# Where key pages, value pages and rows are turned in a decoder layer's attention: inside the projection and the convolutions, or behind them

## The reference

```python
u = modulate(x, 1)
u_pool, q, k_c, v_c, k_s, v_s, k_w, v_w, g_raw = jnp.split(u @ p['w_in'], splits, axis=-1)
kc_full = jnp.concatenate([kc_past, k_c], axis=1)      # past: pages gathered through page_table
vc_full = jnp.concatenate([vc_past, v_c], axis=1)

def compress(k_full, w1, w2, cmp_pos):     # blocks of 32 rows, stride 16
    h = lax.conv_general_dilated(lhs, w_blk, (STRIDE,), 'VALID', dimension_numbers=('NWC', 'WIO', 'NWC'))
    h = h + jnp.einsum('ld,ldh->h', cmp_pos, w_blk)
    return jax.nn.gelu(h) @ w2
```

## Time and profile before

| | us |
|---|---|
| median of 3 runs (lowest, highest) | 1333.18 (1328.6, 1333.52) |
| the profiled execution | 1331.85 |
| its span, first to last instruction | 1330.2 |
| mean granted TensorE clock, share of full | 0.985 |
| input projection, chunks 2 to 14 | 522.9 to 605.5 |
| from there to the end of the value convolution | 605.5 to 670.6 |
| attention loop | 674 to 762 |

### The profile page before, as it was taken

One profiled execution on the slowest core, in us unless ns is written; L12 is line 12 of the kernel. 1 busy time (PEld: TensorE's weight loads), 2 busy tenths in 40 slices (PEclk: granted clock), 3 DMA queues, 4 the chain that ended last, 5 costly groups with the idle time before them and its releaser, 6 DMA issues.

```text
span 1330.2 us, 25199 instructions
## 1 busy us (share of the span) xinstructions
PE 1278.6 (96%) x9736; PEld 1151.1 (87%) x9736; DVE 569.9 (43%) x969; ACT 439.7 (33%) x681; POOL 188.4 (14%) x372
## 2 busy tenths in 40 slices
PE   5999999999999999998988999989999999999997
PEld 3899999999999998996656667979999999988875
DVE  2532222222333366215577775683332332332466
ACT  3322222222211135226456654252222222223343
POOL 3000000000000026552380060142000000030000
PEclk9999999999999998999999999989999999999999
DMA  9545454454342237863740074512223223364463
GB/s 300 157 123 162 127 174 142 133 181 127 108 163 87 79 105 152 183 141 92 225 122 2 12 209 132 174 34 81 80 83 90 79 79 90 90 195 133 147 197 129
DMA packets 217369, 170.15 MB, mean 128 GB/s; under 512 B 47048, under 2 KB 198904, under 8 KB 217225
## 3 DMA queue, kind: packets, MB, share of 16 engines
q1 hardware_dynamic: 210657, 151.37, 39.4%
q0 software_dynamic: 6640, 17.82, 4.7%
HBM read 164.75 MB, written 8.63 MB: 130 GB/s over the span
## 4 chain that ended last, share of the span: by engine, by line
PE 88%; DVE 5%; ACT 3%; issue 1%; DVEq 1%; DMA 1%; SPq 0%; ACTq 0%
PE ps L326 60%; PE ps L925 10%; PE ps L301 3%; PE ps L2472 2%; ACT AR L1868 1%; PE ps L1158 1%; PE ps L1656 1%; PE ps L1765 1%; PE ps L282 1%; DVE AR L2505 1%; PE ps L1673 1%; DVE AR L2033 1%; PE ps L2671 1%; PE ps L1209 1%; PE ps L388 1%
## 5 line engine op out<-in xcount | busy, mean ns | idle before, releaser
L326 PE MATMUL ps<-UH,WH 128*128 128x288 f32 x1648 | 354.6, 296 | 1.0 <-DVE WL L259 1.0
L326 PE MATMUL ps<-UL,WH 128*128 128x288 f32 x1648 | 350.9, 294 | 0.0
L326 PE MATMUL ps<-UH,WL 128*128 128x288 f32 x1648 | 350.3, 293 | 0.0
L259 DVE TENSOR_TENSOR WL<-RAW,WH 128x1024 fp32r<-128x1024 f32 x134 | 164.9, 1231 | 326.4 <-ACT WH L255 322.8
L326 PEld LDWEIGHTS ps<-UH,WH 128*128 128x128 f32 x1648 | 262.9, 188 | 7.4 <-issue 6.2
L326 PEld LDWEIGHTS ps<-UL,WH 128*128 128x128 f32 x1648 | 264.7, 187 | 0.0
L326 PEld LDWEIGHTS ps<-UH,WL 128*128 128x128 f32 x1648 | 263.5, 188 | 0.0
L255 ACT ACTIVATE WH<-RAW 128x1024 fp32r<-128x1024 f32 x134 | 140.8, 1051 | 140.7 <-PE ps L326 134.8
L925 PE MATMUL ps<-WH,H 128*128 128x512 f32 x380 | 97.3, 398 | 0.0
L691 DVE TENSOR_TENSOR T<-MU,ps 128x576 f32<-128x576 f32 x44 | 33.2, 754 | 148.4 <-PE ps L326 144.2
L519 POOL TENSOR_TENSOR AR<-AR 128x576 f32<-128x576 f32 x12 | 19.8, 1647 | 519.6 <-ACT AR L436 457.1
(11 more groups left out here) (377 smaller groups left out, 1506.2 us busy)
## 6 DMA issues: line engine op xcount, KB each, us to landing
RAW<-in_w_ffn_in_dram SPq DMA_DIRECT2D x88, 512.0 KB, 4.0
AW<-in_w_ada_dram SPq DMA_DIRECT2D x42, 512.0 KB, 4.4
RAW<-in_w_ffn_out_dram SPq DMA_DIRECT2D x36, 512.0 KB, 3.6
AR<-in_w_ada_dram SPq DMA_DIRECT2D x7, 1024.0 KB, 11.2
RAW<-in_w_ffn_out_dram SPq DMA_DIRECT2D x16, 448.0 KB, 3.9
AR<-in_w_ada_dram SPq DMA_DIRECT2D x14, 512.0 KB, 6.3
RAW<-in_w_in_dram SPq DMA_DIRECT2D x28, 256.0 KB, 4.3
AW<-in_w_ffn_out_dram SPq DMA_DIRECT2D x14, 512.0 KB, 3.6
```

The lines of the kernel that those rows point to most:

```text
L259: nc.vector.tensor_tensor(WL[:, slot, :], RAW[:, slot, :], WH[:, slot, :].bitcast(F32), ALU.subtract).then_inc(split_done, 1)
L326: mm = nc.tensor.matmul(ps[:, 2 * uslot + h, 0:HT], W[:, wslot, k * P:(k + 1) * P], R[:, k0 + k, h * HT:(h + 1) * HT], start=(first and k ...
```

## The change

- **Key pages.** One set is turned behind each of the chunks 6 to 13 of the projection, into PSUM banks 4 to 7, and copied beside the next chunk. KT8 gets two places: the keys' in the part of AR1 where PG's key places were, the values' where it was. The third place of the split weights moves. The loops over chunks on TensorE and ScalarE are written out.
- **Value pages.** PG has 8 places, for keys and then values. A value set is requested once the keys of its place are turned (`kt_t`): sets 0 to 3 by SP behind the loads of chunks 10 to 13, set 7 by SP behind chunk 14's, sets 4 to 6 by GpSimd behind the keys. They are turned between steps of the key convolution, one set and then two steps, later one (`CONV_STEPS`), into banks 0 to 3.
- **Rows.** All twelve groups are turned inside the value convolution: behind its step 2 (groups 0 to 3), 4 (4 to 7), 6 (8, 9) and 8 (10, 11).
- The prompt blocks are copied during the projection (`prompt_blocks`, now into RS, MU and T2) and multiplied right behind chunk 14; the position row is loaded and turned early. The pool state goes through RAW and is loaded before the bias tables; w_pool is loaded behind the key convolution, since its place now lies under the keys' KT8, as do NAT, KCP, VCP and QB, which GpSimd clears behind it.

The diff, cut to its core:

```diff
@@ attn_sp
-                        ids = page_ids(sp, 2)
-                        for p in range(NPG):
-                            page_load(sp, 1, 2, p, vpg_sp, ids[p])
+                        sp.dma_start(POSN[0:LP, :], cmp_pos[0].rearrange("(l q) d -> l (q d)", q=2)).then_inc(pos_in, 16)
...
+            def value_pages(b):
+                ids = page_ids(sp, b)
+                sp.wait_ge(kt_t, b + 1)
+                for p in range(NPG):
+                    page_load(sp, 1, b, p, vpg_full[b], ids[p])
...
+            for it in range(3):
+                for j in range(2):
+                    c = (it * 2 + j) * P + 1024
+                    columns(it, 8, j, c, c + 64)
+                    if it:
+                        value_pages(2 * it - 2 + j)
...
+            value_pages(NB - 1)
...
-            sp.wait_ge(pconv, 2)
+            sp.wait_ge(conv_done, 1)
@@ attn_pool
-            for kv, nb in ((0, NB), (1, 2)):
...
+            for b in range(NB):
+                ids = page_ids(pool, b)
+                for j in range(NPG):
+                    page_load(pool, 0, b, j, kpg_full[b], ids[j])
+            for b in range(4, NB - 1):
+                ids = page_ids(pool, b)
+                pool.wait_ge(kt_t, b + 1)
+                for j in range(NPG):
+                    page_load(pool, 1, b, j, vpg_full[b], ids[j])
...
-            pool.wait_ge(kt_t, 8)
...
+            pool.wait_ge(conv_done, 1)
+            nc.gpsimd.memset(KCP[:, :], 0.0)
+            nc.gpsimd.memset(VCP[:, :], 0.0).then_inc(kcp_zero, 1)
+            nc.gpsimd.memset(v1["QB"][:, :], 0.0)
@@ attn_pe
+            for it in range(3, 7):
                 for j in range(2):
...
+                    chunk(it, j)
+                    if it == 3 and j == 1:
+                        pe.wait_ge(pos_read, 2)
+                    turn_pages(pe, 0, 2 * it - 6 + j)
...
-            turn_pages(pe, 0)
-            nat_pe(pe, 0, 10)
...
+            prompt_conv(pe, 0)
+            prompt_conv(pe, 1)
+            pe.wait_ge(win_done, 15)
...
+            conv_pe(pe, 0, 0, 4)
             pe.wait_ge(gn_ready, 1)
+            for b in range(NB):
+                turn_pages(pe, 1, b)
+                conv_pe(pe, 0, *CONV_STEPS[b])
...
+            conv_pe(pe, 1, 0, 2)
+            nat_pe(pe, 0, 4)
...
+            conv_pe(pe, 1, 2, 4)
+            nat_pe(pe, 4, 8)
...
+            for q in range(2):
+                conv_pe(pe, 1, 4 + 2 * q, 6 + 2 * q)
+                nat_pe(pe, 8 + 2 * q, 10 + 2 * q)
+            conv_pe(pe, 1, 8, LP)
@@ attn_act
+                elif m == 10:
+                    act.wait_ge(slot_free[1], SL0[a][1] + 6)
+                    prompt_blocks(act, 1)
+                evac(m, m % 2, QSC if 4 <= m < 8 else 1.0, CH0[a] + m)
+                if m >= 6:
+                    compress_evac(act, 0, 0, m - 6, m - 5)
...
-            nat_act(act, 10, 12)
+            nat_act(act, 0, 12)
             act.wait_ge(cx_ready, 1)
@@ attn_dve
+                if j == 9:
+                    dve.wait_ge(slot_free[0], SL0[a][0] + 6)
+                    prompt_blocks(dve, 0)
+                if j >= 6:
+                    compress_evac(dve, 0, 1, j - 6, j - 5)
...
                                     ALU.subtract).then_inc(cx_ready, 1)
+            nat_dve(dve, 8, 12)
@@ places
-        KT8 = v2["KT8"].rearrange("p (g b l j) -> p g b l j", g=NG, b=NB, l=8)
+        KT8 = [v.rearrange("p (g b l j) -> p g b l j", g=NG, b=NB, l=8) for v in (AR1[:, 15 * T:15 * T + NB * PAST], v2["KT8"])]
+        CONV_STEPS = ((4, 6), (6, 8), (8, 10), (10, 12), (12, 13), (13, 14), (14, 15), (15, 16))
...
-        PG = AR1[:, 15 * T:15 * T + 2 * NB * PAST].rearrange("p (s j n) -> p s j n", s=2 * NB, j=NPG // 2)
...
+        PG = AR1[:, 15 * T + NB * PAST:15 * T + 2 * NB * PAST].rearrange("p (s j n) -> p s j n", s=NB, j=NPG // 2)
```

More of the change, by code:

```diff
@@ L1357, in attn_sp @@
                     c = (it * 2 + j) * 64 + 512
-                    columns(it, 4, j, c, c + 256, it + 4)
-            for it0, it1, b in ((0, 2, 6), (2, 3, None)):
-                with sp.Fori(it0, it1) as it:
-                    for j in range(2):
-                        c = (it * 2 + j) * P + 1024
-                        columns(it, 8, j, c, c + 64, None if b is None else it + b)
+                    columns(it, 4, j, c, c + 256)
+            for it in range(3):
[4 more added lines that the diff above has]
+                        value_pages(2 * it - 2 + j)
             wv = w_in[0].rearrange("(k p) n -> p k n", p=P)
@@ L1581, in attn_pe, with chunk @@
             unit_add(pe, FFN_UNITS, 5, RS[:, 0:2 * P], 0)
+            pe.wait_ge(pos_in, 16)
+            nc.tensor.transpose(ps[:, 7, 0:LP], POSN[0:LP, :], IDN[0:LP, 0:LP]).then_inc(pos_t, 1)
+            def chunk(it, j):
+                pe.wait_ge(slot_free[j], SL0[a][j] + 1 + it)
+                product(pe, it * 2 + (CH0[a] + j), (CH0[a] + j) % 2, j, 0, KT, UH, UL, True, True)
             pe.wait_ge(slot_free[0], SL0[a][0] + 2)
             third_product(pe, a)
[L1584 to L1586 removed]
+            chunk(1, 1)
+            for j in range(2):
+                chunk(2, j)
+            for it in range(3, 7):
                 for j in range(2):
[L1588 to L1589 removed]
+                    chunk(it, j)
+                    if it == 3 and j == 1:
+                        pe.wait_ge(pos_read, 2)
+                    turn_pages(pe, 0, 2 * it - 6 + j)
             pe.wait_ge(slot_free[0], SL0[a][0] + 8)
             product(pe, CH0[a] + 14, CH0[a] % 2, 0, 0, KT, UH, UL, True, True)
[L1592 to L1594 removed]
+            pe.wait_ge(phi_full, 32)
             pe.wait_ge(kt_a, 10)
             pe.wait_ge(kt_d, 10)
+            prompt_conv(pe, 0)
+            prompt_conv(pe, 1)
+            pe.wait_ge(win_done, 15)
             for t in range(4):
@@ L1831, in attn_act @@
             scale2_copy(act)
-            for m in range(4):
+            for m in range(14):
                 if m > 1:
                     hi(act, *split_args(a, m + 1))
-                evac(m, m % 2, 1.0, CH0[a] + m)
-            for m0, its, scale in ((4, 2, QSC), (8, 3, 1.0)):
-                with act.Fori(0, its) as it:
-                    for j in range(2):
-                        n, slot, full = split_args(a, m0 + j + 1, it, 2)
-                        hi(act, n, slot, full)
-                        evac(it * 2 + (m0 + j), j, scale, it * 2 + (CH0[a] + m0 + j))
+                if m == 2:
+                    prompt_pos(act, 1)
+                elif m == 10:
[4 more added lines that the diff above has]
+                    compress_evac(act, 0, 0, m - 6, m - 5)
             act.wait_ge(chunk_mm, CH0[a] + 14 + 3)
@@ L2188, in build @@
         pos_t = sem("pos_t")
-        pm_ready = sem("pm_ready")
+        pm_ready = [sem("pm_ready0"), sem("pm_ready1")]
+        pos_read = sem("pos_read")
+        kcp_zero = sem("kcp_zero")
         natp_out = sem("natp_out")
-        kpg_full, vpg_full, vpg_sp = sem("kpg_full"), sem("vpg_full"), sem("vpg_sp")
+        kpg_full, vpg_full = ([sem(f"{n}pg_full{b}") for b in range(NB)] for n in "kv")
         kt_t = sem("kt_t")
@@ L2467, in conv_pe, with turn_pages @@
-        def conv_pe(pe, kv):
-            pe.wait_ge(kt_a, 8 * kv + 10)
-            pe.wait_ge(kt_d, 8 * kv + 10)
-            for l in range(LP):
+        def turn_pages(pe, kv, b):
+            n = 8 * kv + b
+            pe.wait_ge((kpg_full, vpg_full)[kv][b], 16 * NPG)
+            pe.wait_ge(kt_a, n + 1)
+            pe.wait_ge(kt_d, n + 1)
+            for q in range(2):
+                for j in range(4):
+                    mm = nc.tensor.transpose(ps[:, turn_bank(kv, b, q), j * P:(j + 1) * P], PG[:, b, j, q * P:(q + 1) * P], IDN[:, :])
+            mm.then_inc(kt_t, 1)
@@ L2471, in conv_pe, with turn_bank @@
+        def turn_bank(kv, b, q):
+            return 4 * (1 - kv) + 2 * (b % 2) + q
+        def conv_pe(pe, kv, l0, l1):
+            if l0 == 0:
+                pe.wait_ge(kt_a, 8 * kv + 10)
+                pe.wait_ge(kt_d, 8 * kv + 10)
+            for l in range(l0, l1):
                 for g in range(NG):
                     mm = nc.tensor.matmul(ps[64 * g:64 * g + 64, 4 + kv, 0:NB * CS], WPHI[:, kv, l, :],
-                                          KT8[:, g, :, l % 8, l // 8:l // 8 + CS], start=(l == 0), stop=(l == LP - 1))
@@ L2474, in conv_pe, with copy_on, prompt_pos @@
-            mm.then_inc(conv_done, 1)
+                                          KT8[kv][:, g, :, l % 8, l // 8:l // 8 + CS], start=(l == 0), stop=(l == LP - 1))
+            if l1 == LP:
+                mm.then_inc(conv_done, 1)
+        def copy_on(kv, dst, src):
+            if kv:
+                return nc.scalar.activation(dst, src, ACT.Copy)
+            return nc.vector.tensor_copy(dst, src)
+        def prompt_pos(eng, kv):
+            eng.wait_ge(pos_t, 1)
+            for g in range(NG):
+                ev = copy_on(kv, PM[kv][g][:, :, CP], ps[:, 7, 0:LP])
```

(1 more changed line is left out.)

144 lines of the change are left out of this document (41 added, 103 removed).

## The result

The changed kernel takes 1335.84 us (median of 13 runs, 1334.17 to 1340.46), the kernel before, in as many runs beside it, 1330.28 us (1327.45 to 1333.52). The ratio is 1.0048, 95% interval 1.0036 to 1.0060: slower by some 6 us, where the prediction had 1333.0 beside a median of 1333.18, no change. The time lies inside the range, but the case forecast, no change, did not come. The profiled execution has a span of 1335.1 us against 1330.2 us.

A forecast was written before the change was run, and what follows sets the result against it. TensorE, 96% busy, bounds the kernel, so only its idle time can be won. Idle -6.8, seams +1.6 and +1.6, waits +1.0 give -2.6; mixing +3.3 on 1331.85 gives 1332.6, said as 1333 us, range 1327 to 1339.

The forecast's parts named there:

- the case forecast, no change: Whole kernel: 1333 us beside a median of 1333.18, no measurable change; the forecast kept a chance of 0.47.
- What is late next: GpSimd's stores start 31 us later, so its mixing lies wholly beside the attention loop and slows VectorE's scalings: +3.3 us.
- none lands late: SP's moved loads (position row, pool state, w_pool) are each asked for 10 us or more before use: no cost.
- The idle that goes: TensorE's idle time from the input projection's end to the value convolution's end disappears: -6.8 us.
- the new waits: TensorE waits for last value page's copies (0.6), transpose group 11 (0.2), compressed scores' weights (0.2): +1.0 us, ends 0 and 3.
- The seams: TensorE's changes between matmuls and transposes: +1.6 us between projection chunks, +1.6 us behind them, each 0 to 3.2.
- The mixing: GpSimd's pooling work beside the attention loop: extra 18.6 us at 0.18 each cost +3.3 us, ends 0 and 5.7.
- six steps with scalings near 900 ns: Sign of being right: six rather than three attention loop steps have VectorE scalings slowed to near 900 ns.
- rival (c): Every scaling slowed beside GpSimd in the attention loop is on the path: +5.7 for +3.3, 1335 us; chance 0.15.
- SyncE's requests: Value page batches between projection chunks, 9.98 us each with a load, stay hidden with 2.8 us to spare: cost 0.
- Rival (b): SP's batches exceed 10.7 us, chunk 14 of the projection is late, kernel slower: 1338 us at 12 us; chance 0.13.
- What would show it: Trace signs: key pages 1.1 to 1.3 us, value convolution ending near 668, stores near 659, mixing ending beyond 710.

The follow-up runs named there:

- the version that beats both: Changed kernel with state copies behind the gate rows' writes and two pooling row groups turned first, so GpSimd mixes before the other stores: 1325.42 us, ratio 0.9955.

## Why the prediction was wrong

**The step that failed** is "What is late next". The prediction named the right work: GpSimd's stores start 31 us later (658.42, as it said near 659), include two copies of 2 MB, and hold up the two small stores behind them on their own queue. It then followed only GpSimd's queue. On the other queue it asked of each load that the change moves whether it lands in time ("none lands late"), and never looked at loads that the change leaves alone: the bias tables, requested at the end of the value convolution, in the same microseconds as the copies. That is **+7.4 to +8.1 us** by the runs, 6.9 by the traces, with a wait of 6.46 us in it, and the sum had no term for it. The rows to see it were there: the requests in the earlier trace rows, moved by the 31 us of the text, end near 668, and the tables' place in the program is the convolution's end.

On this the Trainium skill would have helped: "DMA: Bandwidth & Descriptors", section "SWDGE vs HWDGE vs iDMA", in the part "Issuing engines are not separate DMA queues", says that requests of all engines end up on the same 16 DMA engines and interleave there. The trace agrees, with both queues in the 16 engines' time at 58.7 and 29.5%; it adds that the issue itself stalls, 15.78 us for eight requests.

**The idle that goes, and the new waits: right.** TensorE's idle time from chunk 2 to the end of the value convolution was 82.66 - 82.62 + 65.04 - 58.26 = 6.8 us and is 52.08 - 51.48 = 0.6 us; the prediction took 6.8 away and put 1.0 back.

**The seams: mis-sized.** Priced at +1.6 between chunks and +1.6 behind, they are 0.3 us together: TensorE's busy time over the same two windows is 140.9 us before and 141.15 after. The row they were priced by, 12 products in 1.79 us with foreign matmuls around them, does not carry over to transposes. The end "0, if the matmuls drain under the transposes" was the right one, and a key page costs 0.87 us, not the 1.1 to 1.3 said. This is why the packing gave 5 to 6 us and not 2.6. That the time still fell inside the range is in part luck: these 2 to 3 us more on one side took off some of the 7 to 8 that were missing on the other.

**The mixing: a cost in the right direction, its size not settled.** +3.3 us predicted, 3.3 to 4.0 by the runs (+-3) and 1.2 by the traces. The price per us was close: 3.1/19.16 = 0.16 us in the kernel with the copies behind the tables, where the prediction took 0.18. But it was read from rows that do not carry it: the first round was set against the second, 24.65 for 20.64, and without mixing the first still takes 21.82, so 1.2 of these 4.0 us were never the mixing's. And no gain at all from leaving the mixing out shows in the runs of the kernel before. If the 3.3 is right, it is so partly by luck. The sign given for it did not come, six steps with scalings near 900 ns: over the first two rounds the 512 wide scalings average 712 ns, and 717 before; the 256 wide ones took 634 for 541. All scalings of the two rounds together are busy 15.8 us for 14.7. The rule of "SBUF — State Buffer" (the Trainium skill, section "SBUF: two separate sides"), that the loser waits for a whole instruction, would give rival (c), +5.7 us; the second round of the kernel with the copies behind the tables, at a clock of 1.00 and with 19.16 us of GpSimd, shows +3.1.

**SyncE's requests: right.** A batch with its load took 9.1 to 10.3 us, predicted 9.98. ScalarE did wait for the loads of chunks 13 and 14, but TensorE did not:

```profile
594.77 1.06 ACT L255 ACTIVATE WH<-RAW 128x1024 fp32r<-128x1024 f32 x1 [0.55 <-DMA RAW<-in_w_in_dram]
...
602.95 1.06 ACT L255 ACTIVATE WH<-RAW 128x1024 fp32r<-128x1024 f32 x1 [1.51 <-DMA RAW<-in_w_in_dram]
```

The chain of waits has all chunks back to back. Rival (b), the slower side, did not happen; the kernel became slower by a mechanism that no rival held.

**What would show it.** Of the marks given, the value convolution's end (665.84, said 668), the stores' start and the mixing's end beyond 710 (722.4) came true, and the clock was 1.00 up to 665. None of them looks at the loop beyond the mixing.

## What to carry to other kernels

When a change shifts a queue's work in time, lay the whole queue at its new place over every other queue's requests, those that the change doesn't touch first, and ask which of them somebody waits for; a bulk copy that nobody needs should be issued where the neighbouring requests have slack, or behind a wait for the one load that has none. Work with a late deadline (here the mixing and the state copies) wants a place of its own in the order, not the place behind whatever produced its neighbour. And a wait can come with more than its length: in each of the six traces in which ScalarE waits over 5 us for the bias table, the granted clock of that round was 0.80 to 0.89. Read the clock of the stretch before the wait is called the whole price.

## What the runs showed of the hardware

- Two copies of 2016 KB from DRAM to DRAM on GpSimd's queue, 14.4 and 14.9 us in flight in the changed kernel, stretch SyncE's issue of eight 64 KB page requests beside them from about 4.4 us to 15.8 (changed kernel), 16.5 (copies ahead of the stores) and 11.8 (copies behind the tables, value pages, 3.8 before). The issuing engine's own program is held, not only the landing; what in the queues holds it is not shown.
- The same copies in the loop's first round, at a DMA share of 0.96, cost the compute engines nothing: 21.81 us, against 21.82 in the kernel before without mixing.
- The granted clock over the first two rounds was 0.83 and 0.93 in the changed kernel (wait 6.46 us), 0.83 and 1.00 in it without mixing (6.10), 0.89 and 0.73 with the copies ahead of the stores (5.84), 0.80 and 0.72 in the kernel before with its copies late (8.08). Without such a wait it was 1.00 and 0.78 with the copies behind the gate rows, 0.93 and 1.00 in that kernel without mixing and in the kernel before, and 1.00 in both rounds of the version that beats both. A lower clock goes with the wait but comes without it too; what lowers it is open.
- Eight float32 transposes between two float32r products cost 0.87 us, 0.109 each, and the products behind them start without a gap; between steps of the key convolution eight of them cost 1.02 us, and eight that had waited for a copy are 1.06 to 1.07 us long.
